# Feed-forward blocks of a two-layer decoder: the order of weight copies, quarter sums, forms and feeds on ScalarE, GpSimd and VectorE

## The reference

```python
# first block
hn = rms_norm(h, norm2_g)
gate, up = jnp.split(hn @ w_gate_up, 2, axis=-1)
h = h + (jax.nn.silu(gate) * up) @ w_down
x = rms_norm(h, final_g)
# second block, at its start and again after its attention
x = x + 0.5 * (jax.nn.silu(rms_norm_2(x, g) @ w_gate) * (rms_norm_2(x, g) @ w_up)) @ w_down
```

## Time and profile before

| | |
|---|---|
| profiled execution | 2016.82 us |
| its span, first to last instruction | 2015.0 us |
| mean granted TensorE clock | 0.990 |
| TensorE busy | 1962.6 us, 97% |
| VectorE, GpSimd, ScalarE busy | 59%, 56%, 47% |
| moved by DMA | 189.68 MB, 94 GB/s |

### The profile page before, as it was taken

The page is one execution under the profiler, slowest core; times in us unless marked ns, Lnnn a source line. Parts: engine busy times, 40 slices in busy tenths (PEclk is TensorE's granted clock), DMA queues, the critical chain, the costliest instruction groups (busy, mean ns, idle before and its releaser), DMA issues.

```text
span 2015.0 us, 30682 instructions
## 1 busy us (share of the span) xinstructions
PE 1962.6 (97%) x11449; PEld 1731.6 (86%) x11449; DVE 1189.4 (59%) x2067; ACT 937.5 (47%) x1649; POOL 1123.3 (56%) x915
## 2 busy tenths in 40 slices
PE   9999999999899999979999999999999989999999
PEld 8998887888689989758898988889888878998987
DVE  6587656545446455765654655676645554646564
ACT  6413235534436435444462644667544453644532
POOL 4445452254567657546666766656555455765753
PEclk9999999999899999989999999999999989999999
DMA  5232321123233333322433333342222323333332
GB/s 181 83 102 87 102 86 51 55 84 105 66 102 106 105 88 102 98 70 79 111 105 100 92 103 105 85 110 78 83 87 84 105 74 94 106 105 97 97 111 84
DMA packets 253850, 189.68 MB, mean 94 GB/s; under 512 B 6608, under 2 KB 249680, under 8 KB 253680
## 3 DMA queue, kind: packets, MB, share of 16 engines
q1 hardware_dynamic: 253024, 187.53, 31.1%
q10 hardware_dynamic: 688, 0.31, 0.1%
HBM read 180.93 MB, written 2.10 MB: 91 GB/s over the span
## 4 chain that ended last, share of the span: by engine, by line
PE 86%; DVE 4%; POOL 4%; ACT 4%; issue 2%; DMA 0%; SPq 0%; DVEq 0%; ACTq 0%
PE ps L793 18%; PE ps L794 18%; PE ps L795 18%; PE ps L944 8%; PE ps L946 8%; PE ps L945 8%; POOL wlo L631 4%; PE ps L1133 1%; PE ps L1285 1%; ACT whi L1350 1%; DVE ps L1892 1%; PE ps L1205 1%; PE ps L1206 1%; PE ps L1207 1%; DVE tmp L1892 1%
## 5 line engine op out<-in xcount | busy, mean ns | idle before, releaser
L631 POOL TENSOR_TENSOR wlo<-raw,whi 128x512 fp32r<-128x512 f32 (+2 forms) x420 | 537.5, 1312 | 579.1 <-ACT whi L1350 433.9
L793 PE MATMUL ps<-xh,whi 128*128 128x512 f32 (+1 forms) x1008 | 383.5, 380 | 31.7 <-POOL wlo L631 31.7
L794 PE MATMUL ps<-xl,whi 128*128 128x512 f32 (+1 forms) x1008 | 375.2, 372 | 0.0
L795 PE MATMUL ps<-xh,wlo 128*128 128x512 f32 (+1 forms) x1008 | 375.1, 372 | 0.0
L1350 ACT ACTIVATE whi<-raw 128x2048 fp32r<-128x2048 f32 (+1 forms) x86 | 160.5, 1867 | 323.7 <-PE ps L795 279.2
L654 POOL TENSOR_TENSOR wlo<-raw,whi 128x512 fp32r<-128x512 f32 x162 | 212.9, 1316 | 160.1 <-ACT whi L1404 160.1
L793 PEld LDWEIGHTS ps<-xh,whi 128*128 128x128 f32 x1008 | 191.2, 190 | 65.0 <-POOL wlo L631 33.8
L795 PEld LDWEIGHTS ps<-xh,wlo 128*128 128x128 f32 x1008 | 190.8, 189 | 33.7
L793 PE MATMUL ps<-fh,whi 128*128 128x512 f32 x528 | 207.9, 394 | 9.2 <-POOL wlo L631 9.2
L794 PEld LDWEIGHTS ps<-xl,whi 128*128 128x128 f32 x1008 | 191.5, 190 | 28.9 <-issue 0.7
L794 PE MATMUL ps<-fl,whi 128*128 128x512 f32 x528 | 206.3, 391 | 0.0
(11 more groups left out here) (386 smaller groups left out, 4991.4 us busy)
## 6 DMA issues: line engine op xcount, KB each, us to landing
raw<-in_w_in SPq DMA_DIRECT2D x87, 512.0 KB, 4.6
raw<-in_w_gate_up SPq DMA_DIRECT2D x44, 512.0 KB, 5.1
raw<-in_ffn_w_gate SPq DMA_DIRECT2D x44, 512.0 KB, 4.0
raw<-in_ffn_w_up SPq DMA_DIRECT2D x44, 512.0 KB, 5.2
raw<-in_ffn_w_down SPq DMA_DIRECT2D x32, 512.0 KB, 4.5
raw<-in_w_down SPq DMA_DIRECT2D x16, 512.0 KB, 4.5
raw<-in_ffn_w_down SPq DMA_DIRECT2D x16, 384.0 KB, 3.8
raw<-in_w_b SPq DMA_DIRECT2D x8, 512.0 KB, 4.0
```

Of the source, the lines that this page charges most:

```text
L631: ins = pool.tensor_tensor(wlo[:, c % 2, cs], raw[:, c % 2, cs], whi[:, c % 2, cs].bitcast(F32), ALU.subtract)
L793: pe.matmul(o, w_of(whi), xhi, start=first, stop=False)
L794: pe.matmul(o, w_of(whi), xlo, start=False, stop=False)
L795: return pe.matmul(o, w_of(wlo), xhi, start=False, stop=last)
```

## The change

On ScalarE a place now copies the next plain or down weights first (`coming(0)`), then takes the silu, and makes the forms after everything for the next chunk. When the next chunk is a down tile after a folded tile, its four pieces are copied two by two at the first two steps. The first quarter sum of weights is rounded after the copy of product 2 and no longer before it. Block 1 has its forms at places 1 and 2 (two sets each); the other blocks keep 0, 1, 1, 2. In the last down group ScalarE feeds the second half of a tile only after the next weight copy, and the last feed comes after the first copy beyond the block. On GpSimd the low half of the activations goes ahead of the next weights only at the first tile of the last group. VectorE rescales block 1's residual one tile at a time. TensorE's down tiles wait for both releases of a folded tile's banks.

```diff
--- before.py
+++ after.py
@@ -75,7 +75,7 @@
 
 
 
-FORMS_AT = {0: (0,), 1: (1, 2), 2: (3,)}
+FORMS_AT = ({0: (0,), 1: (1, 2), 2: (3,)}, {1: (0, 1), 2: (2, 3)})
 
 
 STEPS, _n = [], 0
@@ -665,11 +665,11 @@
                     if folded(p + 1):
                         fold_low(f, p + 1)
                         continue
-                    if down_part(p) is not None and up_tile(p - 1) is not None:
+                    if down_part(p) == (2, 0):
                         act_low(f, p - 1)
                     if p + 1 < FFN_LEN:
                         low(C_F[f] + p + 1)
-                    if down_part(p) is None and up_tile(p - 1) is not None:
+                    if down_part(p) != (2, 0) and up_tile(p - 1) is not None:
                         act_low(f, p - 1)
 
             piece = 2 * P
@@ -979,7 +979,7 @@
                 k0 = sum(DOWN_K[:r])
                 pe.wait_ge(w_lo, c + 1)
                 for t in range(2):
-                    pe.wait_ge(acc_free, 2 * (c - 2) + t + 1)
+                    pe.wait_ge(acc_free, 2 * (c - 2) + (2 if folded(p - 2) else t + 1))
                     for k in range(DOWN_K[r]):
                         if j == 0 and t == 0:
                             pe.wait_ge(h_split, FK * f + k0 + k + 1)
@@ -1416,8 +1416,8 @@
                     corner_high(0, 0, 0)
                 elif z == 1:
                     corner_high(1, 1, 1)
+                elif z == 2:
                     sum_high(4, 0)
-                elif z == 2:
                     sum_high(5, 1)
                 else:
                     corner_high(2, 1, 0)
@@ -1450,9 +1450,10 @@
 
                         if folded(p + 1):
                             fold_high(f, p + 1, z)
-                        elif folded(p):
-                            high_piece(c + 1, z)
-                        elif p and z == 0:
+                        elif folded(p) and z < 2:
+                            high_piece(c + 1, 2 * z)
+                            high_piece(c + 1, 2 * z + 1)
+                        elif p and z == 0 and not folded(p):
                             high(c + 1)
 
                     def kept(dst, src, level):
@@ -1461,14 +1462,9 @@
                             act.activation(dst[:], src, ACT.Copy).then_inc(prod_kept, 1)
 
                     r1, r5, _ = fold_out(c)
-                    if n is not None and not folded(p - 1):
-                        act.wait_ge(acc_free, 2 * (c - 1) + 1)
-                        act.activation(tmp[:, 1, :], tmp[:, 0, :], ACT.Silu).then_inc(silu_done, 1)
-                    for i in FORMS_AT.get(p, ()):
-                        fold_forms(f, i, own)
                     coming(0)
-                    if folded(p - 1):
-                        act.wait_ge(acc_free, 2 * c)
+                    if n is not None:
+                        act.wait_ge(acc_free, 2 * c if folded(p - 1) else 2 * c - 1)
                         act.activation(tmp[:, 1, :], tmp[:, 0, :], ACT.Silu).then_inc(silu_done, 1)
                     kept(prod1, r1, 1)
                     coming(1)
@@ -1479,12 +1475,15 @@
                         act.activation(fh[:, n % RING, :], tmp[:, 3, :], ACT.Copy).then_inc(h_hi, 1)
                     kept(prod6, r1, 3)
                     coming(3)
+                    for i in FORMS_AT[f == 1].get(p, ()):
+                        fold_forms(f, i, own)
                     if down_part(p) is not None and down_part(p)[0] == 2:
-                        for t in range(2):
-                            m = 2 * down_part(p)[1] + t
+                        for m in range(max(2 * down_part(p)[1] - 1, 0), 2 * down_part(p)[1] + 1):
                             act.wait_ge(h_new, 3 * DK * f + 2 * DK + m + 1)
                             feed(S + 1, m, gain)
                 high(C_F[f] + FFN_LEN + 1)
+                act.wait_ge(h_new, 3 * DK * (f + 1))
+                feed(S + 1, DK - 1, gain)
 
             def project(c, S, gain):
                 with act.Fori(0, 2) as i:
@@ -2057,11 +2056,6 @@
                         dve.tensor_tensor(tmp[:, 0, :], ps[:, bank(c, 0), :], rsx, ALU.mult).then_inc(acc_free, 1)
                         continue
                     r, j = down_part(p)
-                    if f == 1 and (r, j) == (0, 0):
-                        for n in range(DK):
-                            x = hT[:, n, META:TM]
-                            stt(x, x, vec[:, V_FIN + n:V_FIN + n + 1], ssum[:, META:TM], ALU.mult, ALU.mult).then_inc(xn_done, 1)
-                        dve.wait_ge(xn_done, DK)
                     if (r, j) == (2, 0):
                         clear(S + 1)
                         if S + 1 == 2:
@@ -2070,6 +2064,9 @@
                     for t in range(2):
                         m = 2 * j + t
                         x = hT[:, m, META:TM]
+                        if f == 1 and r == 0:
+                            stt(x, x, vec[:, V_FIN + m:V_FIN + m + 1], ssum[:, META:TM], ALU.mult, ALU.mult).then_inc(xn_done, 1)
+                            dve.wait_ge(xn_done, m + 1)
                         done(c, t)
                         dve.wait_ge(h_done, FK * f + sum(UPS[:r + 1]))
                         if f or r or m:
```

## The result

The changed kernel takes **1972.58 us** (median of four runs, 1970.78 to 1973.02) against 2016.88 of the kernel before (four runs beside it, 2016.38 to 2017.62): a ratio of 0.9778, 95% interval 0.9761 to 0.9795. The forecast was 1971.3. The profiled execution took 1973.02 us (span 1971.1), 43.8 less than the 2016.82 of before.

The account below looks back on a forecast made before the run. TensorE, busy 97%, was taken as the bound, its waits and lower clock costing 58.8 us. Terms 36.1 + 7.3 + 1.9 - 1.1 + 1.3 - 0.2 = 45.3 us took 2016.6 to 1971.3 us; range 1958 to 1986.

Parts of the forecast that it names:

- block starts: Start of each feed-forward block: copying weights before silu and forms gains 36.1 us of 37.9 lost with the clock.
- second down tiles: Second down tile of each block: GpSimd's next weights ahead of the activations' low half gain 7.3 us.
- pieces: Next down weights copied two by two in the last folded tile: three of six 0.36 us stops go, gain 1.9 us.
- product copies: Folded tiles after down tiles: 6.1 us of stops become 1.9 at five places and 5.3 at the sixth, sum -1.1.
- first seam: End of first block: three stops (3.7 us) go, but the late last feed delays the sums; gain 1.3 us.
- later seams: The two other seams: room is 2.3 us and the shift takes 2.4, a loss of 0.1 us each.
- Third tiles: Third tile of each block and what follows: waits left are 0.9 + 0.2 + 0.6, called 1.8 us.
- the rival of 1992: Wait moves to the fourth tiles, some 5 us plus 1.9 of clock in each block, 21 us: 1992; chance 0.07.
- the sixth: Second block's first folded tile after down tiles: two rescales in VectorE's queue delay the fifth product; 5.3 us left with clock.
- The rival "everything goes" (1958): All 58.8 us of waits go, VectorE's delay absorbed at the seam and in the second block: 1958; chance 0.13.
- The rival of 1980: VectorE beside GpSimd costs more: 1.78 us per rescale, seam loses gain and clock, one block start too: 1980; chance 0.15.
- The slower rival: ScalarE becomes the bound of the 54 folded tiles, 0.95 us each, 51 us: 2023; chance 0.03.

Follow-up runs that it names:

- experiment 5: Changed kernel with ScalarE's old order at block starts: silu and forms ahead of the weights' copy, sets at 0, 1, 1, 2 in every block; 2007.26 us.
- Experiment 6: Changed kernel with GpSimd's low half of the activations ahead of the next weights at the first tile of every down group again; 1976.57 us.
- experiment 1: Changed kernel with the second block's eight rescales back in one go at its first down tile; 1968.43 us.
- experiment 12: Changed kernel with edits of experiments 2, 3 and 4, plus silu and activations' copy ahead of the weights' copy before the last group; 1960.29 us.
- experiment 2: Changed kernel with the eight rescales spread over the first three down tiles and none at the fourth; 1968.77 us.
- Experiment 9: Changed kernel with GpSimd held at the seams until VectorE's chain is done, ScalarE's order untouched; 1966.79 us.
- experiment 3: Changed kernel with the last feed ahead of the first weight copy beyond the block, in all three blocks; 1967.09 us.
- experiment 10: Changed kernel with ScalarE's old feeds: both halves before the next weight copy, last feed before the first copy beyond the block; 1971.57 us.
- experiment 4: Changed kernel with one set of forms at place 1 and three at place 2 in all blocks; 1969.36 us.
- experiment 7: Changed kernel with one piece of the next down weights at each of the last folded tile's four steps again; 1972.80 us.
- experiment 8: Changed kernel with the first quarter sum rounded ahead of the copy of product 2 again; 1976.74 us.

## Why the prediction was right, and which terms of it were not

Both kernels issue the same 11449 multiplications in the same order, so the starts of the two profiled executions can be set side by side. The changed kernel is 0.65 us behind from the first 10 us on, where the change touches nothing, and 0.75 behind at 500 us, ahead of the first third tile. At the end it is 43.9 ahead: 44.6 us gained in the blocks and at their seams, against 45.3 in the sum. By term, with the forecast in brackets: block starts 35.9 (36.1), second down tiles 7.4 (7.3), pieces 1.9 (1.9), product copies 0.1 (-1.1), first seam 2.3 (1.3), later seams -2.9 (-0.2). The first three terms were right, mechanism and size. That the total is right to a microsecond is partly luck: the last three miss by 1.2, 1.0 and -2.7, which nearly cancel. The terms in turn:

- **Third tiles: 1.8 left by the forecast, 2.2 measured.** The first block leaves 1.0 (0.9 forecast) and the third nothing. In the second block 0.8 was expected, split between a start and a later folded tile; it came as one stop at the fourth tile, 1.24. The step took the silu chain there at its old length, while VectorE's product of the norm factors went from 0.69 to 1.73 us beside the subtractions moved there; that this is the cause is read from the timeline and was not tried by itself. The edit's worth is shown by experiment 5 (34.7 us; 36.1 forecast), and the rival of 1992 with 5 us stops at the fourth tiles is out: the only stop at one is 0.98.
- **Second down tiles: 7.3 us, all gone.** Experiment 6 gives back 4.0 of them, as its rescales are spread (stops of 1.05, 1.50, 1.05). The other 3.3 came from the burst beside it: experiment 1 has the burst back, with GpSimd's new order, and no stop there.
- **Pieces: 1.9 us, as forecast,** three of six stops, and the other three at the eighth slice. The excess there is 0.82 each, as before. What makes the slice late is ScalarE's copy of the next weights ahead of the silu: experiment 12 moves it, and the stops go.
- **Product copies.** At five places the left is 0.45 or 0.33, as forecast. At the sixth I gave 5.3 us and it is 4.0 (stop 2.35, restart 0.24, clock 1.4). The two rescales took 0.80 and 1.78, together the 2.6 of the sum, though neither took its 1.3. Too high were the 0.5 for the add and the 0.2 for waits: the two adds took 1.90 together, and 2.18 where no rescale stands beside them (experiment 2). So the chain was 2.2 us late and not 3.3, and the clock cost 1.4 instead of 1.7. That this place loses is shown by experiments 1 and 2, which remove it. By the rule of the Trainium skill that was weighed there (SBUF — State Buffer, "Who interferes with whom") each rescale would have taken nearer 1.8 us, and the stop would have been 1 us longer: one of the two did, and the stop was shorter.
- **First seam: 2.4 us left forecast, 1.5 measured** (stops of 0.47 and 0.55 with what follows them). The wait for the last x slice did not come.
- **Later seams: the mis-sized term.** I took 0.1 us each, and each has a stop of 1.32, 1.6 with its restart. The room was 2.3 us and the step put the shift at 2.4. It was 3.8 at the second seam: the last x slice starts 0.35 us later, and then x slice, sum of squares, cast and subtraction take 0.45, 1.08, 0.97 and 0.96 more (0.75, 0.69, 0.43 and 0.69 became 1.20, 1.77, 1.40 and 1.65). The prediction names only adds and sums of squares as what gets longer beside GpSimd; the add at these seams did not (0.69), and the cast and the subtraction were left out. Experiment 9 shows it by taking only GpSimd away.

The rival "everything goes" (1958) names what the change could reach: experiment 12 comes to 1960.3 by putting four steps elsewhere. The rival of 1980 had the right quantity, VectorE beside GpSimd, but not the place: one rescale did take 1.78, while the first seam kept its gain and its clock, and the loss came at the later seams. The slower rival never began: no folded tile but the named ones has a stop.

**What stays open** is when the clock falls. After the same stop of about 2.35 us it fell in the profiled executions of the changed kernel and of experiments 3, 5, 6, 9 and 10 (0.64 to 0.66 over the next 4.9 us), and not in those of 4 and 7. It even stayed up after 2.99 us in experiment 8. That is worth 1.4 us. The changed kernel's fastest run, 1970.78, has a mean granted clock of 1.000 and its three others, about 2 us longer, have 0.999; that this is the same stop is likely but was not traced. Effects of a microsecond or two were therefore read from the excess of TensorE, not from the time. TensorE's stricter wait for free banks was not tried by itself; no stop in the trace points to it.

## What to carry to other kernels

Account for the bounding engine stop by stop, each with its restart and the clock behind it; of the six edits that were undone here one was worth 35 us. When a weights' copy moves forward, ask which subtraction on GpSimd it sets off and which VectorE chain then runs beside it: where something waits for that chain's end, put the copy behind it or hold GpSimd. And when one edit removes the harm of a burst, look whether a second edit against the same burst still pays; here it cost 4 us.

## What the runs showed of the hardware that I had not expected

- A cast with a single input, 128x512 from f32 to fp32r, is slowed as well: 0.43 us alone, 1.40 beside GpSimd's subtractions. The slow-down is mutual: four subtractions took 6.10 us against 5.03. Where a rescale lost little (0.80), it was GpSimd that lost: its subtraction from 945.00 on took 1.75 us, and 1.29 in experiment 2, where no rescale stands beside it. The Trainium skill (SBUF — State Buffer, "Who interferes with whom") says that casts, too, can take the port pair that VectorE shares with GpSimd. These rows agree; applied to the cast at the seams, it would have shown part of the mis-sized term.
- A rescale or add of the same shape cost 0.80, 0.95 or 1.78 us within six microseconds: GpSimd was busy through nearly all of it, so one number per instruction is only a mean.
- The same stop of about 2.35 us is followed by 1.2 GHz in some kernels' executions and by 2.4 GHz in others (28 and 39 multiplications in some 4.8 us), and even one of 2.99 us was once followed by 2.4 GHz.
